# Stick-breaking attention heads in steps of one block of 128 keys for two heads

## The reference, cut to what matters

```python
def stick_breaking_attention(h, w_qkv, w_o):
    ...
        z = jnp.einsum('bqhd,bshd->bhqs', q_blk, k).astype(jnp.float32) * scale
        causal = key_pos[None, :] < t[:, None]
        log_1m = jnp.where(causal, jax.nn.log_sigmoid(-z), 0.0)
        excl = lax.cumsum(log_1m, axis=3, reverse=True) - log_1m
        a = jnp.where(causal, jnp.exp(jax.nn.log_sigmoid(z) + excl), 0.0)
        return jnp.einsum('bhqs,bshd->bqhd', a.astype(v.dtype), v)
```

## Time and profile before

| | us |
|---|---|
| median of 3 runs | 2533.39 (2528.71 to 2534.61) |
| the profiled execution | 2534.2 |
| its span, first to last instruction | 2532.4 |
| heads' stage, first score product to last value product | 1089.8 to 1236.5 |
| PE busy | 2453.5 (97%) |
| DVE, ACT, POOL busy | 1315.4, 819.3, 203.4 |
| mean granted TensorE clock | 0.978 of full speed |

### The profile page before, as it was taken

How to read it: one execution, slowest core, us unless ns; L and a number is a source line. 1 busy time by engine, 2 the same in 40 slices (tenths; PEclk the granted TensorE clock), 3 DMA queues, 4 the chain that set the end, 5 groups by cost and what they waited for, 6 DMA issues and landing times. The chain is left out here.

```text
span 2532.4 us, 28747 instructions
## 1 busy us (share of the span) xinstructions
PE 2453.5 (97%) x11404; PEld 1909.7 (75%) x11404; DVE 1315.4 (52%) x2191; ACT 819.3 (32%) x1342; POOL 203.4 (8%) x190
## 2 busy tenths in 40 slices
PE   7999999999999999989999999999999999999998
PEld 6778788768888878866788888877645456888887
DVE  4766455454444443368555454644466663545553
ACT  2333544233222222257432222321433442322222
POOL 1301320000000000023100000101200000000001
PEclk8999999999999999989999999999899999999999
DMA  4233114213333322300123333332200002233331
GB/s 131 75 101 91 34 59 150 75 51 91 95 97 96 96 92 83 92 25 1 42 83 98 94 100 92 92 98 73 84 1 1 1 1 59 86 98 93 99 96 46
DMA packets 290981, 188.08 MB, mean 74 GB/s; under 512 B 7840, under 2 KB 284576, under 8 KB 290848
## 3 DMA queue, kind: packets, MB, share of 16 engines
q1 hardware_dynamic: 290128, 184.31, 24.2%
q10 hardware_dynamic: 720, 1.95, 0.2%
HBM read 184.14 MB, written 2.10 MB: 74 GB/s over the span
## 5 line engine op out<-in xcount | busy, mean ns | idle before, releaser
L464 DVE TENSOR_TENSOR wl<-raw,wh 128x1024 fp32r<-128x1024 f32 x336 | 412.0, 1227 | 753.2 <-ACT wh L454 752.3
L468 PE MATMUL ps<-xb_x,wh 128*128 128x512 f32 (+1 forms) x2000 | 620.9, 392 | 0.0
L454 ACT CAST wh<-raw 128x1024 fp32r<-128x1024 f32 x336 | 349.1, 1040 | 802.9 <-PE ps L468 792.4
L468 PEld LDWEIGHTS ps<-xb_x,wh 128*128 128x128 f32 (+1 forms) x2000 | 373.6, 187 | 79.8
L468 PE MATMUL ps<-xb_x,wl 128*128 128x512 f32 (+1 forms) x1000 | 392.2, 392 | 0.0
L468 PE MATMUL ps<-XH,wh 128*128 128x512 f32 x680 | 274.1, 403 | 3.1 <-DVE mz_prev L1095 2.4
L468 PE MATMUL ps<-XL,wh 128*128 128x512 f32 x680 | 268.5, 395 | 0.0
L468 PE MATMUL ps<-XH,wl 128*128 128x512 f32 x680 | 268.1, 394 | 0.0
L468 PEld LDWEIGHTS ps<-xb_x,wl 128*128 128x128 f32 (+1 forms) x1000 | 187.2, 187 | 44.1
L533 POOL TENSOR_TENSOR sq<-H 128x512 f32<-128x512 f32 x64 | 68.5, 1071 | 1714.0 <-DVE H L583 1636.8
L468 PEld LDWEIGHTS ps<-XH,wh 128*128 128x128 f32 x680 | 130.0, 191 | 31.3 <-DVE mz_prev L1095 3.3
(11 more groups left out here) (329 smaller groups left out, 3649.8 us busy)
## 6 DMA issues: line engine op xcount, KB each, us to landing
raw<-in_mlp_w SPq DMA_DIRECT2D x128, 512.0 KB, 3.7
raw<-in_w_gate_up SPq DMA_DIRECT2D x44, 512.0 KB, 3.7
raw<-in_w_in SPq DMA_DIRECT2D x29, 512.0 KB, 3.6
raw<-in_sb_w_qkv SPq DMA_DIRECT2D x24, 512.0 KB, 3.6
raw<-in_w_down SPq DMA_DIRECT2D x22, 512.0 KB, 3.4
raw<-in_w_out_mix SPq DMA_DIRECT2D x16, 512.0 KB, 3.3
raw<-in_w_kv SPq DMA_DIRECT2D x16, 512.0 KB, 3.8
raw<-in_nsa_w_kv SPq DMA_DIRECT2D x12, 512.0 KB, 3.4
```

The costliest lines, as they stand in the source:

```text
L454: e.copy(shaped(WH[i % NH], i), shaped(RAW[i % NR], i)).then_inc(*w_hi.up(i))
L464: e.tensor_tensor(shaped(WL[i % NH], i), shaped(RAW[i % NR], i), shaped(WH[i % NH], i).bitcast(F), ALU.subtract).then_inc(*w_lo.up(i))
L468: return e.matmul(out, a, b, start=start, stop=stop, skip_group_check=True)
```

## The change

A step is now one block of keys for the two heads of a pair: `ST` lists 32 steps, pair by pair, j = 3, 2, 1, 0. A step takes two PSUM banks (one a head) out of six, so three steps have room. The two heads' products follow one another, one on partitions 0 to 63, the other on 64 to 127 (for the values: output rows 0 to 63 and 64 to 127). The mask is added right behind the scores, before softplus, so masked places give L = 0 and the 0/1 products go. The absolute value is always made by DVE, as a bitwise and on int32; ACT's Abs and DVE's 2 max(z, 0) - z go. For j = 0 and 1 the two heads are handled apart (`parts`), for j = 2 and 3 in one instruction. `Lh` and `Ll` get a buffer for each j (two for j = 3).

PE's order in round n is cum(n-2), out(n-3), scores(n). ACT's is exp and ln of step n, then the weights of step n-2. DVE's is abs(n), `Ll` of n-1, max and add of n. POOL rounds step n.

```diff
+    ST = [(c, j) for c in range(8) for j in (3, 2, 1, 0)]
+    NST = len(ST)
+    Lp = Ring([Buf(ph.sb(f"L{i}", [128, 2, 512])) for i in range(4)])
+    Lh = [Ring([Buf(ph.sb(f"Lh{j}{i}", [128, 2, wd[j]], R)) for i in range(2 if j == 3 else 1)]) for j in range(4)]
+    Ll = [Ring([Buf(ph.sb(f"Ll{j}{i}", [128, 2, wd[j]], R)) for i in range(2 if j == 3 else 1)]) for j in range(4)]
+
+    def parts(n):
+
+        return [slice(0, 1), slice(1, 2)] if ST[n][1] < 2 else [slice(0, 2)]
+
+    def heads_of(part):
+        return range(2)[part]
...
+        pairs = Ring([0, 1, 2])
+        for n in range(NST):
+            c, j = ST[n]
+            at = pairs.next()
+            for m in range(2):
+                plan(PS[2 * at + m], ("sk", n, m), (a_made, ("sw", n, m)))
+            plan(Lp.next(), ("L", n), (mixed, ("so", n)))
+            last = 4 * c + 3
+            plan(Lh[j].next(), ("Lh", n), (scored, ("cum", last)))
+            plan(Ll[j].next(), ("Ll", n), (scored, ("cum", last)))
+            if j == 3:
...
-            mm(e, t[:, o:o + 128], Ib[:, :], maskb[:, 2, :], False, False)
...
+        bk = [take(e, ("sk", n, m))[:, 0:wd[j]] for m in range(2)]
+        for m in range(2):
+            p0 = 64 * m
+            mm(e, bk[m], k_s[p0:p0 + 64, c, 128 * j:128 * j + 128], q_s[p0:p0 + 64, c, 128 * j:512], True, False)
+        for m in range(2):
+            mm(e, bk[m][:, 0:128], Ib[:, :], maskb[:, 2, :], False, False).then_inc(*scored.up("z", n, m))
...
+            e.wait_ge(*v_made.at("lo", n, part.start))
+            for m in heads_of(part):
+                t = got(("sk", n, m))
+                for i in range(j, 4):
+                    hb, lb = got(("Lh", 4 * c + 3 - i)), got(("Ll", 4 * c + 3 - i))
+                    out = t[:, 128 * (i - j):wd[j]]
+                    by = trir[:, 0 if i == j else 1, :]
+                    mm(e, out, by, hb[:, m, :], False, False)
+                    f = mm(e, out, by, lb[:, m, :], False, i == 3)
+                f.then_inc(*(scored.up("cum", n) if m else scored.up("cum0", n)))
...
+        e.wait_ge(*a_made.at("sw", n, 1))
+        for m in range(2):
+            h = 2 * c + m
+            f = mm(e, o[64 * m:64 * m + 64, 128 * j:512], v_s[:, j, 64 * h:64 * h + 64], L[:, m, 0:wd[j]], j == 3,
+                   j == 0)
+        f.then_inc(*mixed.up("so", n))
...
-        for h in range(16):
-            pe_stick_scores(e, h)
-            if h >= 2:
-                pe_stick_out(e, h - 2)
-            if h >= 1:
-                pe_stick_cum(e, h - 1)
-        pe_stick_out(e, 14)
-        pe_stick_cum(e, 15)
-        pe_stick_out(e, 15)
+        for n in range(NST + 3):
+            if 2 <= n < NST + 2:
+                pe_stick_cum(e, n - 2)
+            if n >= 3:
+                pe_stick_out(e, n - 3)
+            if n < NST:
+                pe_stick_scores(e, n)
...
+        def weights_of(n):
+            L, j = got(("L", n)), ST[n][1]
+            for m in range(2):
+                e.wait_ge(*scored.at("cum" if m else "cum0", n))
+                e.activation(L[:, m, 0:wd[j]], got(("sk", n, m))[:, 0:wd[j]], ACT.Exp).then_inc(*a_made.up("sw", n, m))
+
+        for n in range(NST + 2):
+            if n < NST:
+                c, j = ST[n]
+                L = got(("L", n))
+                for part in parts(n):
+                    e.wait_ge(*v_made.at("abs", n, heads_of(part)[-1]))
+                    e.activation(L[:, part, 0:wd[j]], L[:, part, 0:wd[j]], ACT.Exp, scale=-1.0).then_inc(
+                        *a_made.up("exp", n, part.start))
+                for part in parts(n):
+                    e.wait_ge(*a_made.at("exp", n, part.start))
+                    e.activation(L[:, part, 0:wd[j]], L[:, part, 0:wd[j]], ACT.Ln, bias=ONE1).then_inc(
+                        *a_made.up("ln", n, part.start))
+            if n >= 2:
+                weights_of(n - 2)
...
-            for n in (1, 2):
-                f = e.activation(L[:, sl(n)], got(("sk", h, n))[:, 0:W[n]], ACT.Abs)
...
-        for n in (1, 2, 0):
-            if n:
-                e.wait_ge(*a_made.at("ln12", h))
-                f = e.scalar_tensor_tensor(l[:, sl(n)], got(("sk", h, n))[:, 0:W[n]], 0.0, l[:, sl(n)], ALU.max, ALU.add)
-            else:
-                e.wait_ge(*a_made.at("ln0", h))
-                f = e.tensor_tensor(l[:, 0:512], l[:, 0:512], a[:, :], ALU.add)
-            f.then_inc(*v_made.up())
-            e.wait_ge(*v_made.now())
-            for j in range(4):
-                if BK[j] == n:
-                    f = e.tensor_tensor(l[:, OFF[j]:OFF[j] + 128], l[:, OFF[j]:OFF[j] + 128], con("MS"), ALU.mult)
-            f.then_inc(*v_made.up("sm", h) if n == 0 else v_made.up("sm", h, n))
-            e.wait_ge(*v_made.now())
-            if n != 1:
...
+    def dve_stick_abs(e, n):
+        L, w = take(e, ("L", n)), wd[ST[n][1]]
+        for m in range(2):
+            e.wait_ge(*scored.at("z", n, m))
+            e.tensor_scalar(L[:, m, 0:w].bitcast(I32), got(("sk", n, m))[:, 0:w].bitcast(I32), 0x7FFFFFFF, None, ALU.bitwise_and).then_inc(
+                *v_made.up("abs", n, m))
+
+    def dve_stick_terms(e, n):
+
+        L, w = got(("L", n)), wd[ST[n][1]]
+        for m in range(2):
+            e.wait_ge(*a_made.at("ln", n, m if len(parts(n)) == 2 else 0))
+            e.scalar_tensor_tensor(L[:, m, 0:w], got(("sk", n, m))[:, 0:w], 0.0, L[:, m, 0:w], ALU.max,
+                                   ALU.add).then_inc(*v_made.up("sp", n, m))
+
+    def dve_stick_lo(e, n):
+        L, w = got(("L", n)), wd[ST[n][1]]
+        hi, lo = got(("Lh", n)), take(e, ("Ll", n))
+        for part in parts(n):
+            e.wait_ge(*g_made.at("hi", n, part.start))
+            e.tensor_tensor(lo[:, part, :], L[:, part, 0:w], hi[:, part, :].bitcast(F), ALU.subtract).then_inc(
+                *v_made.up("lo", n, part.start))
...
-            e.tensor_scalar(l[:, 0:512], z0[:, :], 0.0, None, ALU.max).then_inc(*v_made.up())
-            e.wait_ge(*v_made.now())
-            e.scalar_tensor_tensor(a[:, :], l[:, 0:512], 2.0, z0[:, :], ALU.mult, ALU.subtract).then_inc(
-                *v_made.up("sabs", h))
-        dve_stick_terms(e, 15)
-        out(13)
...
+        for n in range(NST + 1):
+            if n < NST:
+                dve_stick_abs(e, n)
+            if n >= 1:
+                dve_stick_lo(e, n - 1)
+            if n < NST:
+                dve_stick_terms(e, n)
...
+        for n in range(NST):
+            L, hi, w = got(("L", n)), take(e, ("Lh", n)), wd[ST[n][1]]
+            for part in parts(n):
+                e.wait_ge(*v_made.at("sp", n, heads_of(part)[-1]))
+                e.tensor_scalar(hi[:, part, :], L[:, part, 0:w], 1.0, 0.0, ALU.mult, ALU.add).then_inc(
+                    *g_made.up("hi", n, part.start))
```

More of the change, by code:

```diff
@@ L7 @@
 BF = mybir.dt.bfloat16
+I32 = mybir.dt.int32
 ALU = mybir.AluOpType
@@ L1763, in plan_stick @@
         plan_spread("one")
-        six = Ring(PS[0:6])
-        six.i = psr.i
-        for h in range(16):
[L1767 to L1774, removed]
+        pairs = Ring([0, 1, 2])
[9 more added lines that the diff above has]
+            if j == 3:
+                plan(PS[6 + c % 2], ("so", c), (x_lo, ("so", c)))
         for o in range(8):
@@ L1777, in plan_stick, with pe_stick_scores @@
         plan_next("m")
-    def pe_stick_scores(e, h):
-        p0, c = 64 * (h % 2), h // 2
-        bk = [take(e, ("sk", h, n)) for n in range(3)]
+    def pe_stick_scores(e, n):
+        c, j = ST[n]
         e.wait_ge(*v_made.at("sqk", c))
         e.wait_ge(*v_made.at("sqk", 8 + c))
[L1784 to L1798, removed]
-            mm(e, t[:, o:o + 128], Ib[:, :], maskb[:, 2, :], False, False)
[L1800 to L1805, removed]
@@ L1817, in pe_stick, with pe_stick_out @@
+    def pe_stick_out(e, n):
+        c, j = ST[n]
+        L, o = got(("L", n)), take(e, ("so", c)) if j == 3 else got(("so", c))
+        e.wait_ge(*a_made.at("tok", "sv1", 3))
+        e.wait_ge(*a_made.at("sw", n, 1))
[4 more added lines that the diff above has]
+        f.then_inc(*mixed.up("so", n))
     def pe_stick(e):
@@ L1890, in act_stick @@
                 e.activation(H[:, k, :], H[:, k, :], ACT.Copy, scale=col("first", k)).then_inc(*a_made.up("first", k))
[L1891 to L1908 removed]
+            if n >= 7 and n % 4 == 3:
+                out(n // 4 - 1)
+        out(7)
         a_.end("heads_st")
@@ L1978, in dve_stick @@
         dve_diag(e, "one")
[L1980 to L1998 removed]
+        for n in range(NST + 1):
[5 more added lines that the diff above has]
+                dve_stick_terms(e, n)
+            if n >= 7 and n % 4 == 3:
+                c = n // 4 - 1
+                dve_lo(e, X, "so", c, got(("so", c))[:, :])
+        dve_lo(e, X, "so", 7, got(("so", 7))[:, :])
         v_.end("heads_st")
@@ L2016, in pool_stick @@
     def pool_stick(e):
-        for h in range(16):
-            if h >= 1:
-                pool_stick_hi(e, h - 1)
-            if 3 <= h < 11:
```

(14 more changed lines are left out.)

83 lines of the change are left out of this document (10 added, 73 removed).

## The result

The changed kernel takes 2584.98 us (median of 4 runs, 2583.06 to 2591.93), the kernel before it 2534.0 us on the same chip; the ratio of their runs is 1.0219, with a 95% interval from 1.0197 to 1.0242 (the two medians alone give 1.020). So it is slower beyond doubt, by some 2%. The forecast was 2589, in a range from 2550 to 2612, and slower. Where executions were disturbed, with a lower clock in the whole program (two of the four of e6, at 2671 and 3224 us, are the worst), the numbers of the experiments are those of the undisturbed ones.

The account below looks back on a forecast made before the run. PE was taken to bound the kernel before, and a serial loop through PE, DVE and ACT the new stage: 2534 + 23 (loop) + 30 (half clock) = 2587, 2589 with the slow start; range 2550 to 2612.

Parts of the forecast that it names:

- The loop at full clock: Heads' stage: each step walks serially through PE, DVE, ACT and PE; 20.8 us a pair instead of 17.1, +23 us.
- One sign: Profile after, heads' stage: before nearly every score product PE idles until ACT's weights exp; no size given.
- The clock: Heads' stage: PE at 1.2 GHz half of the time, 30 us a pair there against 20.8; +30, 32 with the start.
- Nothing else in the program moves: Outside the heads' stage of 146.9 us: no change; the output projection starts the same way behind the last value product.
- Column halves: Two heads' value products: full overlap taken, nearest row being the row halves; without it 2.13 us more a pair, +17.
- DVE's bitwise and: Absolute value on int32, no row: between 0.425 us for 256 columns and half of it; half would give back 10 us.
- The engines' own sums: Work per pair of heads: DVE 11 to 12 us, ACT 11; if these decided, a pair would take 12 to 13.
- The clock stays full: Rival, heads' stage: full clock behind the start, 2557 us; chance 17%.
- The value products don't overlap: Rival, heads' stage: 2.1 us more a pair with somewhat less half clock, 2600 us; chance 24%.
- Half clock throughout: Rival, heads' stage: half clock all the time, stage 248 against 147, 2635 us; chance 6%.
- Faster, the loop is not closed: Rival, heads' stage: the busiest engine sets the pace, 12.5 us a pair, 2497 us; chance 6%.

Follow-up runs that it names:

- e6: Changed kernel with both heads' scores on the same row half of the array (values wrong, same work): 2623.9 us.
- e9: Changed kernel with products of 128x512 added behind every step's scores and a second behind the 384-step's sums, to keep the clock full: 2550.2 us.
- the orders' runs: Changed kernel with ACT's weights moved ahead of exp and ln, PE's scores moved ahead of sums and value products, or both: 2553.4, 2540.2, 2502.0 us.
- e11: Changed kernel with the added products that keep the clock full, and both heads' value products on the same column half: 2571.7 us.
- e10: Changed kernel with ACT's and PE's orders both changed, and the 256-step's exp and ln between the 512-step's two heads' weights; second execution: 2498.8 us.
- e5: Changed kernel with both heads' value products on the same column half of the array (values wrong, same work): 2602.4 us.

## Why the prediction came out

Step by step, in the order of its text:

- **The loop at full clock.** It can be read from e9, where one pair runs from 1175.20 to 1196.06. The rows (added products, masks, splits and sums left out) are the terms of the sum:

```profile
1175.20 0.70 PE L469 MATMUL ps<-st_q,st_k 64*128 64x256 f32 x4
...
1176.17 0.76 DVE L1925 TENSOR_SCALAR st_L<-ps 128x256 int32<-128x256 int32 x2 [3.52 <-PE ps L469]
...
1176.96 0.63 ACT L1893 ACTIVATE st_L<-st_L 128x512 f32<-128x512 f32 x1 [4.16 <-DVE st_L L1925]
...
1184.91 1.13 PE L469 MATMUL ps<-st_q,st_k 64*128 64x512 f32 x4
...
1186.31 1.29 DVE L1925 TENSOR_SCALAR st_L<-ps 128x512 int32<-128x512 int32 x2 [1.56 <-PE ps L469]
...
1187.03 1.23 ACT L1893 ACTIVATE st_L<-st_L 128x512 f32<-128x512 f32 x2 [2.55 <-DVE st_L L1925]
...
1190.08 0.65 PE L469 MATMUL ps<-st_L,st_v 128*64 128x256 f32 x4
1190.66 0.49 PE L469 MATMUL ps<-st_q,st_k 64*128 64x128 f32 x4
...
1195.27 0.87 PE L469 MATMUL ps<-st_L,st_v 128*64 128x384 f32 x4
1196.06 0.70 PE L469 MATMUL ps<-st_q,st_k 64*128 64x256 f32 x4
```

| term, us a pair | forecast | measured |
|---|---|---|
| scores and mask, up to the start of the absolute value | 3.85 and some 0.2 of hand-overs | 4.32 |
| absolute value, up to ACT (in the 128-step, its end) | 2.5 | 2.59 |
| ACT, three steps, up to the value products | 7.8 | 7.84 |
| 128-step: splits and sums | 3.4 | 3.36 |
| value products, up to the next scores | 2.75 | 2.75 |
| sum | 20.8 with 0.5 of hand-overs | 20.86 |

The 256-step gives 0.97 (1175.20 to 1176.17), 0.79 and 2.41 (to the value products at 1179.37), the 512-step 1.40, 0.72 and 3.05 (to 1190.08), and so on for the others. The stage was put at 170 and took 169.6, its +23 came as 22.7. In the changed kernel itself the step at full clock took 5.18 us, as in e9, and the one ahead of it, which began at half clock, 5.68 against 5.40. This step was right, term by term, and the orders' runs show that it is the cause. One sign was put too strongly: PE was to wait for ACT's weights before nearly every score product, and it did so 9 times, since elsewhere the sums end at about the same time, or later at half clock.

- **The clock.** The price was about right and the share was not. Forecast: 9.2 us more for a pair that is at half clock for 30 us, so 0.31 per us; measured 0.30. But I took half of the time, and it was 62% of the stage. With that share a pair would have been put at 25.7 (0.62 of the time at a rate of one pair in 30 us, the rest at one in 20.8), and it took 26.4 on average behind the first (those pairs have a clock of 0.68, and the price by them alone is 0.33). The term was 32 with the start, and 38 came. The mis-sized term is the assumption "at 1.2 GHz for half of its time", which no row of before could fix.

- **The parts outside.** "Nothing else in the program moves" was right for the instructions and wrong for the time: 12.1 us came off there in the profiled executions, and 5.8 of them are what two executions of one code differ by. So that the total came as close as 2589 against 2585 is partly luck: the stage was 6 us longer than the forecast's 202.

- **What no row showed.** Column halves: full overlap, as taken; e11 puts its price at 2.11 us a pair. In the changed kernel's rows it is the four 512-column passes in 1.08 us at 1193.73, where four in a row would take 1.7. The sentence of the Trainium skill, page "TensorE: Matmul & The Clock Gate", section "Part 3: Packing small matmuls", by which loads overlap only across row groups, does not hold for these products: all rows are shared, and the trace has all four loads in the first 0.20 us from 1193.73 on, with the first products already running. DVE's bitwise and: the bound of half the price fell; it costs what the other reads of PSUM cost (0.68 for 512 columns in the earlier trace rows), as the groups by form of the changed kernel show for 512 and 128 columns (busy us, mean ns, idle before):

```profile
L1920 DVE TENSOR_SCALAR st_L<-ps 128x512 int32<-128x512 int32 x16 | 10.3, 686 | 25.2 <-PE ps L469 25.2
...
L1920 DVE TENSOR_SCALAR st_L<-ps 128x128 int32<-128x128 int32 x16 | 3.9, 286 | 16.2 <-PE ps L469 16.2
```

- **The engines' own sums.** DVE's two sets of eight were put at 7.8 us and ACT at 11; DVE is busy for 86 us in the stage, 10.8 a pair (forecast 11 to 12), and ACT for 85, 10.6. Sums like these come near to the bound only when the loop is open, and then it is PE's: of a pair's 13.87 us in e10 PE is busy for 12.77, DVE for 10.46 and ACT for 9.90.

- **Rivals.** "The clock stays full" would have given 2557, and its stage, 169.6, is what e9 measured; what spoke against it, the half clock that followed thin stretches in the earlier trace rows, decided. "The value products don't overlap" fell by e11. "Half clock throughout" (2635) fell with 0.69. "Faster, the loop is not closed" was put at 2497 with ACT's and PE's orders against it; with both orders turned 2502.0 came, and 2498.8 with the heads' weights parted as well.

## What to carry to other kernels

Before a stage is cut into finer steps, follow one step through all engines and ask what stands ahead of it in each engine's order: the steps made DVE's work in the stage smaller, 86 us instead of 109, and the stage 61 us longer, because each queue held other steps' work in front of the link that the next engine was waiting for. Put at the head of each engine's round what the others are waiting for: here the older step's last exp on ACT, and on PE the scores, which need only a free bank. And count the clock with the loop: a chain that leaves PE gaps pays twice (here 22.7 and 38.3 us), and one test for it is to add products that do nothing.

## What the runs showed that I had not expected

- Adding work made the program faster, which I came to expect only when the first trace showed the clock: 36 products, two passes of 512 columns each, took 35 us off (2585.0 to 2550.2).
- Making PE do the same work in a slower arrangement can raise the clock (e5: 0.81 against 0.69) or lower it (e6: 0.61). The price of an overlap, read from such a run alone, is 9 or 39 us of stage where it is 16 to 20 with added products.
- Two executions of one code differ by 5.8 us before they reach the changed stage, so a changed stage is best compared by its own length.
